# Token-major GLA output in a two-layer encoder kernel, with extra transposes behind it and at the head, a reordered start and eleven warm-up matmuls

## The reference

```python
for l in range(DEPTH):
    x = x + 0.5 * swiglu(rmsnorm(x, ffn1_norm[l]), ...)          # D_FF = 2816
    x = x + hybrid_mixer(rmsnorm(x, mix_norm[l]), ...)
    x = x + 0.5 * swiglu(rmsnorm(x, ffn2_norm[l]), ...)
return rmsnorm(x, final_norm)

# in hybrid_mixer, proj = h @ w_in, split into q_a k_a v_a q_g k_g v_g gate_lr r_g
attn = rmsnorm(sliding_window_attention(q_a, k_a, v_a, attn_sinks), attn_out_norm)
o = gla_chunked(q_g, k_g, v_g, log_a)       # per chunk: masked (q_e k_e^T) v + q_e S
o = rmsnorm(o, gla_out_norm) * silu(r_g)    # the norm is over one head's 128 columns
return concat([attn, o]) @ w_out
```

## Time and profile before

| | us |
|---|---|
| runs of the kernel: median (lowest, highest), 3 runs | 936.03 (930.25, 936.21) |
| the profiled execution, as a run | 929.8 |
| its span, first to last instruction | 928.2 |
| PE busy | 920.3 (99%) |
| DVE busy | 607.1 (65%) |
| ACT busy | 454.8 (49%) |
| POOL busy | 3.5 |
| DMA: 169.06 MB, mean | 182 GB/s |

### The profile page before, as it was taken

The page is one execution under the profiler, slowest core; times in us unless marked ns, Lnnn a source line. Parts: engine busy times, 40 slices in busy tenths (PEclk is TensorE's granted clock), DMA queues, the critical chain, the costliest instruction groups (busy, mean ns, idle before and its releaser), DMA issues.

```text
span 928.2 us, 19280 instructions
## 1 busy us (share of the span) xinstructions
PE 920.3 (99%) x8130; PEld 913.3 (98%) x8130; DVE 607.1 (65%) x701; ACT 454.8 (49%) x498; POOL 3.5 (0%) x7
## 2 busy tenths in 40 slices
PE   9999999999999999999999999999999999999997
PEld 9999999999999999999999999999999999999996
DVE  7765565688768665555686655567796785565554
ACT  7444444457746444444554344446675644444443
POOL 0000000000000000000000000000000000000001
PEclk9999999999999999999999999999999999999999
DMA  8675655563246655655556555655613665655531
GB/s 284 235 233 189 210 181 193 178 204 108 75 163 220 224 183 185 202 193 188 181 196 218 183 184 188 214 182 143 223 47 92 227 227 184 213 191 181 199 118 46
DMA packets 130997, 169.06 MB, mean 182 GB/s; under 512 B 3344, under 2 KB 116752, under 8 KB 130960
## 3 DMA queue, kind: packets, MB, share of 16 engines
q1 hardware_dynamic: 130384, 167.86, 54.9%
q10 hardware_dynamic: 576, 0.66, 0.2%
HBM read 167.46 MB, written 1.05 MB: 182 GB/s over the span
## 4 chain that ended last, share of the span: by engine, by line
PE 96%; DVE 1%; DMA 1%; ACT 1%; SPq 0%; issue 0%; POOLq 0%; DVEq 0%
PE ps L380 30%; PE ps L382 30%; PE ps L381 30%; PE ps L630 1%; PE ps L643 1%; DMA raw<-in_ffn_w_down 1%; DMA resid<-in_xt 1%; DVE wlo L1137 1%; PE ps L468 0%; PE ps L767 0%; PE ps L790 0%; PE ps L777 0%; DVE xlo L1126 0%; PE ps L725 0%; PE ps L702 0%
## 5 line engine op out<-in xcount | busy, mean ns | idle before, releaser
L1121 DVE TENSOR_TENSOR wlo<-raw,whi 128x2048 fp32r<-128x2048 f32 x157 | 351.3, 2238 | 237.4 <-ACT whi L863 237.4
L380 PE MATMUL ps<-xhi,whi 128*128 128x256 f32 x1648 | 457.6, 278 | 0.0
L381 PE MATMUL ps<-xlo,whi 128*128 128x256 f32 x1648 | 455.2, 276 | 0.0
L382 PE MATMUL ps<-xhi,wlo 128*128 128x256 f32 x1648 | 455.2, 276 | 0.0
L863 ACT ACTIVATE whi<-raw 128x2048 fp32r<-128x2048 f32 (+2 forms) x158 | 295.8, 1873 | 145.1 <-PE ps L382 141.9
L380 PEld LDWEIGHTS ps<-xhi,whi 128*128 128x128 f32 x1648 | 309.4, 188 | 1.8 <-issue 1.0
L381 PEld LDWEIGHTS ps<-xlo,whi 128*128 128x128 f32 x1648 | 309.5, 188 | 0.0
L382 PEld LDWEIGHTS ps<-xhi,wlo 128*128 128x128 f32 x1648 | 309.5, 188 | 0.0
L380 PE MATMUL ps<-h_parts,whi 128*128 128x256 f32 x768 | 212.4, 277 | 0.1
L381 PE MATMUL ps<-h_parts,whi 128*128 128x256 f32 x768 | 212.1, 276 | 0.0
L382 PE MATMUL ps<-h_parts,wlo 128*128 128x256 f32 x768 | 212.1, 276 | 0.0
(11 more groups left out here) (168 smaller groups left out, 500.4 us busy)
## 6 DMA issues: line engine op xcount, KB each, us to landing
raw<-in_ffn_w_down SPq DMA_DIRECT2D x44, 1024.0 KB, 4.7
raw<-in_ffn_w_gate SPq DMA_DIRECT2D x42, 1024.0 KB, 5.2
raw<-in_ffn_w_up SPq DMA_DIRECT2D x42, 1024.0 KB, 5.2
raw<-in_w_in SPq DMA_DIRECT2D x12, 1024.0 KB, 5.0
raw<-in_w_in SPq DMA_DIRECT2D x8, 512.0 KB, 4.3
raw<-in_w_out SPq DMA_DIRECT2D x8, 512.0 KB, 4.3
raw<-in_w_in SPq DMA_DIRECT2D x2, 1088.0 KB, 5.1
raw<-in_w_out SPq DMA_DIRECT2D x8, 256.0 KB, 3.8
```

The costliest lines, as they stand in the source:

```text
L380: pe.matmul(o, w_hi, x_hi, start=start, stop=False, skip_group_check=True)
L381: pe.matmul(o, w_hi, x_lo, start=False, stop=False, skip_group_check=True)
L382: return pe.matmul(o, w_lo, x_hi, start=False, stop=stop, skip_group_check=True)
L1121: nc.vector.tensor_tensor(lo, r, h.bitcast(F32), ALU.subtract).then_inc(lo_done, 1)
```

## The change

- `WARM`: 11 warm-up matmuls instead of 16.
- The first norm: six transposes (`spread` three times into bank 5, which nobody reads) stand ahead of the two that are read.
- First down unit: ACT runs silu first, then splits the unit in two halves with the high part of the hidden activations between; DVE makes the low part of the hidden activations ahead of both halves.
- GLA output, token-major: R0 and R1 by `project_tokens`; silu directly from PSUM on ACT, with the norm's factor as its scale; the products of scores and v, and those of the states, with their operands swapped, so o is token-major; squares with an accumulated sum on ACT instead of copies, squares and PE's column sums; one DVE product per head and token tile for factor and gate; eight transposes back to feature-major into banks 0 and 3; the gain goes into the high and low parts.
- Eight transposes (`spread` with `SETTLE`) that nobody reads stand behind those eight.
- End: tiles 4 and 5 to 7 are scaled one square later.

```diff
-WARM = 16
+WARM = 11
 SETS = 4
+SETTLE = 8
...
-        o32 = work[:, 4:8, :]
+        o_tok = work[:, 4:8, :].rearrange("p (t a) c -> p t (a c)", t=TT)
+        o_sq = sq[:, 4:8, :].rearrange("p (t a) c -> p t (a c)", t=TT)
+        sg_tok = sg[:, :, :].rearrange("p (t a) c -> p t (a c)", t=TT)
+        def o_tile(tt, h):
+            return ps[1 + h % 2][:, tt * UC + h // 2 * P:tt * UC + (h // 2 + 1) * P]
...
+                        for _ in range(3):
+                            spread([ps[5]], 0, rs_y, TT)
...
-                project(M_R0, t, tiles(0), attention_sums)
-                def o_tile(h):
-                    return tiles(1 + h % 2)[:, h // 2, :]
+                project_tokens(M_R0, t, [ps[0][:, 0:UC], ps[0][:, UC:2 * UC]], attention_sums)
                 pe.wait_ge(kg_ev, ev)
-                for h in range(GH):
-                    j = h // 2
-                    for tt in range(TT):
-                        pe.matmul(o_tile(h)[:, tt * P:(tt + 1) * P], vg[:, tt, h * P:(h + 1) * P],
-                                  AT[:, 4 * (h % 2) + 2 * j + tt, :],
-                                  start=(h < 2 and tt == 0), stop=False, skip_group_check=True)
+                for tt in range(TT):
+                    for h in range(GH):
+                        pe.matmul(o_tile(tt, h), AT[:, 4 * (h % 2) + 2 * (h // 2) + tt, :], vg[:, tt, h * P:(h + 1) * P],
+                                  start=tt == 0 and h < 2, stop=False, skip_group_check=True)
                 spread([ps[3][:, 256:512]], 5 * l + 2, rs_y, TT).then_inc(rA_ps, 1)
                 pe.wait_ge(st_done, 5 * ev)
-                for j in range(2):
-                    for c in range(1, NCH):
-                        for h in (2 * j, 2 * j + 1):
-                            b = DK * (h % 2)
-                            last = pe.matmul(o_tile(h)[:, c * CHUNK:(c + 1) * CHUNK], Sta[b:b + DK, c - 1, j, :],
-                                             qe[b:b + DK, j, c * CHUNK:(c + 1) * CHUNK],
-                                             start=False, stop=True, skip_group_check=True)
-                            if j == 1 and c == NCH - 1:
-                                last.then_inc(o_ps, 1)
-                def gla_sums():
-                    pe.wait_ge(am_done, 4 * l + 2)
-                    for h in (0, 2, 1, 3):
-                        if h < 2:
-                            pe.wait_ge(osq_done, 2 * l + h + 1)
-                        for tt in range(TT):
-                            last = pe.matmul(ps[3][:, 2 * h + tt:2 * h + tt + 1],
-                                             sq[:, 4 + h, tt * P:(tt + 1) * P], ones[:, 0:1],
-                                             start=True, stop=True, skip_group_check=True)
-                    last.then_inc(oss_done, 1)
-                pe.wait_ge(rg_ev, 2 * l + 1)
-                project(M_R1, t, tiles(0), gla_sums)
+                for c in range(1, NCH):
+                    for h in range(GH):
+                        j, b, r = h // 2, DK * (h % 2), CHUNK * (c % 2)
+                        last = pe.matmul(o_tile(c // 2, h)[r:r + CHUNK, :], qe[b:b + DK, j, c * CHUNK:(c + 1) * CHUNK],
+                                         Sta[b:b + DK, c - 1, j, :], start=False, stop=True, skip_group_check=True)
+                        if c == NCH - 1 and h >= 2:
+                            last.then_inc(o_ps, 1)
+                pe.wait_ge(sg_done, 4 * l + 2)
+                project_tokens(M_R1, t, [ps[0][:, 0:UC], ps[0][:, UC:2 * UC]])
                 pe.wait_ge(at_ev, 2 * ev)
                 for i in range(M_WO, MU - 1):
...
                     last.then_inc(unit_done, 1)
                     if i == M_WO + 1:
-                        pe.wait_ge(o_ev, 2 * ev)
-                        spread([ps[1], ps[2]], 5 * l + 3, rs_y, 8).then_inc(rG_ps, 1)
+                        pe.wait_ge(og_done, 2 * ev)
+                        for h in range(GH):
+                            for tt in range(TT):
+                                last = pe.transpose(ps[3 * (h // 2)][:, (h % 2 * TT + tt) * P:(h % 2 * TT + tt + 1) * P],
+                                                    o_tok[:, tt, h * P:(h + 1) * P], ident)
+                            if h % 2:
+                                last.then_inc(og_ps, 1)
+                        spread([ps[1], ps[2]], 5 * l + 3, rs_y, SETTLE)
...
+            def half_hi(ft):
+                act.wait_ge(loaded[1], 16)
+                act.wait_ge(unit_done, ST + 2)
+                c = slice(ft * D, (ft + 1) * D)
+                nc.scalar.activation(whi[:, 1, c], raw[:, 1, c], ACT.Copy).then_inc(hi_done if ft else half_up, 1)
...
-                split_hi(1, t + 1)
-                silu(grp)
-                h_hi(0, grp)
+                    split_hi(1, t + 1)
+                    silu(grp)
+                    h_hi(0, grp)
+                else:
+                    silu(0)
+                    half_hi(0)
+                    h_hi(0, 0)
+                    half_hi(1)
...
+                def gate_out(i):
+                    act.wait_ge(unit_done, ST + 3 * t + i + 1)
+                    c = UC * (i == M_R1)
+                    for tt in range(TT):
+                        nc.scalar.activation(sg_tok[:, tt, c:c + UC], ps[0][:, tt * UC:(tt + 1) * UC], ACT.Silu,
+                                             scale=rcol[:, tt:tt + 1]).then_inc(sg_done, 1)
+                gate_out(M_R0)
                 split_mix(10)
-                act.wait_ge(rg_ev, 2 * l + 1)
-                nc.scalar.activation(sg[:, 0:2, :], sg[:, 0:2, :], ACT.Silu).then_inc(sg_done, 1)
 ...
-                for b in range(2):
-                    act.wait_ge(o_ps, 2 * l + b + 1)
-                    nc.scalar.copy(o32[:, b:4:2, :], tiles(1 + b)).then_inc(o_ev, 1)
-                    act.wait_ge(o_ev, 2 * l + b + 1)
-                    nc.scalar.activation(sq[:, 4 + b:8:2, :], o32[:, b:4:2, :],
-                                         ACT.Square).then_inc(osq_done, 1)
+                for p in range(2):
+                    act.wait_ge(o_ps, 2 * l + p + 1)
+                    for h in (p, p + 2):
+                        for tt in range(TT):
+                            e = nc.scalar.activation(o_sq[:, tt, h * P:(h + 1) * P], o_tile(tt, h), ACT.Square,
+                                                     accum_out=osum[:, GH * tt + h:GH * tt + h + 1])
+                    e.then_inc(osq_done, 1)
+                gate_out(M_R1)
                 split_mix(11)
-                act.wait_ge(rg_ev, 2 * ev)
-                nc.scalar.activation(sg[:, 2:4, :], sg[:, 2:4, :], ACT.Silu).then_inc(sg_done, 1)
                 split_mix(12)
                 split_mix(13)
                 for b in range(2):
-                    act.wait_ge(am_done, 4 * l + b + 3)
-                    mixed_hi(xhi[:, 4 + 2 * b:6 + 2 * b, :], o32[:, 2 * b:2 * b + 2, :])
+                    act.wait_ge(og_ps, 2 * l + b + 1)
+                    nc.scalar.activation(xhi[:, 4 + 2 * b:6 + 2 * b, :], tiles(3 * b), ACT.Copy,
+                                         scale=par[:, G_GLA:G_GLA + 1]).then_inc(mhi_done, 1)
                 split_mix(14)
...
-                if n < 3:
-                    for m in ms:
-                        scaled(m)
-            scaled(6)
-            scaled(7)
+                for m in ((0, 1), (2, 3), (), (4,), (5, 6, 7))[n]:
+                    scaled(m)
...
                     fourth_lo(3)
+                    h_lo(0, 0)
                     half_lo(0)
-                    h_lo(0, 0)
                     half_lo(1)
...
-                done(M_R0)
-                nc.vector.tensor_tensor(sg[:, 0:2, :], tiles(0), r_tiles(2), ALU.mult).then_inc(rg_ev, 1)
...
-                dve.wait_ge(oss_done, ev)
-                nc.vector.tensor_scalar(rs_v[:, :], ps[3][:, 0:8], EPS * P, None, ALU.add).then_inc(eps_in, 1)
+                dve.wait_ge(osq_done, 2 * ev)
+                nc.vector.tensor_scalar(rs_v[:, :], osum[:, :], EPS * P, None, ALU.add).then_inc(eps_in, 1)
                 dve.wait_ge(eps_in, ev)
                 rsqrt(5 * l + 3, rs_v[:, :], 8, P, rs_y[:, 0:8])
-                done(M_R1)
-                nc.vector.tensor_tensor(sg[:, 2:4, :], tiles(0), r_tiles(2), ALU.mult).then_inc(rg_ev, 1)
+                dve.wait_ge(rs_step, RS * (5 * l + 4))
+                dve.wait_ge(sg_done, 4 * ev)
+                for tt in range(TT):
+                    for h in range(GH):
+                        c = slice(h * P, (h + 1) * P)
+                        e = nc.vector.scalar_tensor_tensor(out=o_tok[:, tt, c], in0=o_tile(tt, h),
+                                                           scalar=rs_y[:, GH * tt + h:GH * tt + h + 1],
+                                                           in1=sg_tok[:, tt, c], op0=ALU.mult, op1=ALU.mult)
+                    e.then_inc(og_done, 1)
                 split_mix(11)
-                dve.wait_ge(sg_done, 2 * ev)
```

(19 more changed lines are left out.)

28 lines of the change are left out of this document (14 added, 14 removed).

## The result

| | before | after |
|---|---|---|
| runs beside each other: median (lowest, highest) | 933.1 (929.8, 936.2), 4 | 952.5 (949.3, 956.2), 4 |
| the profiled execution, as a run | 929.8 | 956.2 |
| its span | 928.2 | 954.1 |
| PE busy | 920.3 | 946.1 |

The ratio is 1.021, with an interval of 1.014 to 1.028: the change makes the kernel about 2% slower. The same kernel in another session gave 953.1 against 936.1 (four runs of it, 25 of before; 1.016, interval 1.009 to 1.024). The ratios in this document leave out runs that took over 1.5% more than the fastest of their kernel, so they can stand nearer to 1 than the ratio of two medians.

The account below looks back on a forecast made before the run. TensorE, 96% of the chain that ended last, was taken to bound the kernel. Terms of -3.58, +1.75, -0.92, +0.65, -0.14 and -0.1 summed to -2.3, taking 929.8 to 927.5; range 925.5 to 934.

Parts of the forecast that it names:

- state matmuls: Mixer: still twelve, with 64x64 stationary and 128 streaming columns; 1.28 becomes 0.82, -0.46 a layer, -0.92 in all.
- this term: R projections, now token-major: slow pace charged to their 96 passes and 48 output passes behind them, +0.65.
- Both waits of the head: PE waits at 28.49 (0.17) and 30.23 (0.37) in the first FFN, both claimed to go.
- the lead of 0.25: Head: five fewer warm-up matmuls let PE start piece 2 earlier, a lead of 0.25 after the restart.
- The tail: Kernel end: scaling of tiles 4 and 5 no longer stands ahead of tile 6's square; -0.1.
- Transposes: Mixer: eight added transposes of the gated output cost +0.87 a layer, +1.75; unread spreads replace read ones at no cost.
- Head: Kernel start: earlier start, six added transposes, two waits gone, -0.14; eight transposes in a row expected to help the pace.
- E: Rival: sixteen transposes leave PE slow, second FFN of both layers slow, 941; or the clock falls, 970; 5%, 1 for clock.
- C: Rival: the pace does not settle in most runs, one FFN is slow at +6.5; 932.5 to 934.5; 20%.
- D: Rival: a new wait from the gating chain, the split behind it or late hidden activations; 928.6 to 930; 10%.
- B: Rival: R projections keep the fast pace (-1.3) or state matmuls reach their bound (-0.3); 925.5 to 926.9; 20%.
- The reading of the medians: The two longer runs of the kernel before were inferred to have a slow first FFN, 6.0 against a measured 5.9.

Follow-up runs that it names:

- the one with tiny matmuls: Changed kernel plus one unread fp32 matmul of 16 rows by 32 columns in six places, behind mixer transposes and ahead of FFN loops; median 930.6, ratio 0.9965.

## Why the prediction was wrong

*The sum was nearly right.* Each term can be read off: column sums gone; transposes +0.88 a layer (forecast 0.87); state matmuls 0.82 (0.82). R1 was fast in layer 0 and slow in layer 1, the output units behind it slow in both; the forecast had all 144 passes of each layer slow, and took 72 of them as slow before where layer 1 of before has 96. So this term is +0.3 in all, where +0.65 was taken. R1 in layer 0 also shows that activations as the stationary operand don't fix the pace. The products ran from 265.25 to 267.41, 2.3 ahead of the transposes (forecast 1.7), with the squares at 0.25 where 0.39 was taken and the products at 0.27 where 0.35 was; the split behind them ended at 270.75, before the transposes did. Both waits of the head went: no two starts of PE between 24.2 and 34 us are more than 0.125 apart. But of the lead of 0.25 only 0.07 was left behind the two new waits: the stretch behind the spreads starts at 23.91, with the six transposes (0.65) ahead of it, where it was 23.33. That makes the head +0.04 (forecast -0.14), and even this is within its scatter: with the same head, that start moves between 23.36 and 24.37 over the traces. The tail, from the last pass of the stream to the end of the span, went from 10.3 to 10.0 (forecast 0.1). With the slow passes taken out, 927.0 stands against 927.5.

*The step that failed* is the one under "Transposes" and "Head" that took the eight transposes of the earlier trace rows for the cause of the fast pace behind them, and so left the pace of the FFNs out of the sum, at nothing. It came to 29.2 in the profiled run: 6.6 for the first FFN and about 22.5 for all that stands behind the mixers' transposes. I had one event of that kind in either layer, and charged it to the nearest instruction. The runs put the condition in what stood ahead: the column sums, which the sum entered as 1.79 a layer of pure gain. Undone alone, they bring the changed kernel to 931.0 without a slow FFN; done alone, they take the kernel before to 951.3. The gain of 3.6 was real and bought a loss of 22.5 behind the transposes. For the first FFN's 6.6 no cause is shown: it is slow in some runs of either kernel. What in the engine sets the pace stays open too.

*The rivals.* E named what happened, both second FFNs slow behind the transposes, and the point from which it decides, but gave it 4 in 100, stopped at two FFNs (941), and named a cause, the sixteen, that the runs refute. It stopped at two for no reason in the rows: in the trace of before the pace held across the column sums ahead of an FFN, and a mixer's last units lead through two such breaks to the second and the next first FFN. C's objection, that no row shows what flips the pace, was the honest state of knowledge, and deserved most of the chance; its size, one FFN, was the narrow part. D did not happen, and B only in R1 of layer 0. The clock stayed at 1.00 behind sixteen transposes (window at 272.0). The Trainium skill ("TensorE: Matmul & The Clock Gate", Part 4: PE-mode transpose) says that transposes don't count as PE-busy for the clock in the way matmuls do. Sixteen in a row, 1.67 us, brought no fall of the granted clock here.

*The reading of the medians* holds: runs of variants at 936.9 and 936.4 (of the kernel before) and 935.5 (of the changed one) were profiled, and in each the first FFN alone is slow. No trace of the unchanged kernel in such a run was taken. What the reading missed is that these three runs, two of them with a slow FFN, showed a pace drawn anew in each execution. A change that moves instructions around such a draw can't be costed from one trace at either pace.

## To carry to other kernels

Where a kernel is all TensorE, take its time apart into passes times the price of a pass, stretch by stretch, before and after: a granted clock of 1.00 does not say that the price is the lowest. If runs differ by equal steps, find the stretch whose price makes that step, and forecast a change as a distribution over its states. Work removed from a long stream also removes an interruption, so time the removal alone, with that part of the computation left out, before the rest is built on it.

## What the runs showed of the hardware

- Two stable paces for one and the same stream of 128x256 passes, 113.3 and 117.8 ns from start to start, at a granted clock of 1.00 both; each held for 1,500 passes and more. It changed behind other work of PE and, from R1 to the output units at 264.10, between two streams of the same shape, of which one has the activations as the stationary operand and the other the weights. In the slow pace the starts stand 117 to 119 ns apart, and the weight loads of the third product last 191 ns instead of 188 (group L389 of the changed kernel against the one with tiny matmuls):
```profile
L389 PEld LDWEIGHTS ps<-xhi,wlo 128*128 128x128 f32 x1584 | 302.3, 191 | 0.0
```
```profile
L389 PEld LDWEIGHTS ps<-xhi,wlo 128*128 128x128 f32 x1584 | 297.5, 188 | 0.0
```
- The pace behind a break depends on what stood ahead of the break too, and in most places on chance: the kernel before spread its 124 runs over five levels.
- An unread fp32 matmul of 16 rows by 32 columns costs 0.53 in such a stream. Its two passes start 0.13 apart, with 0.20 from the start ahead of them to the first and from the second to the next; two of 128 columns cost 0.8.
